# Three low parts of activation combinations moved from VectorE to GpSimd in the first feature group

## The reference

```
    h = h + jnp.concatenate([conv_out, ret_out], axis=-1) @ w_out
    f = jnp.square(jax.nn.relu(rmsnorm(h, norm_ffn_w) @ w_up)) @ w_down
    return h + f, new_hist, new_state.astype(h.dtype)
```

## Time and profile before

| what | value |
|---|---|
| time, median of 3 runs | 1175.36 us (1175.01 to 1176.11) |
| time of the profiled execution | 1177.58 us |
| its span in the profile | 1175.8 us |
| busy PE, PEld | 1161.0 us (99%), 1061.5 us (90%) |
| busy DVE, ACT, POOL | 931.1 us (79%), 548.0 us (47%), 379.9 us (32%) |

### The profile page before, as it was taken

How to read it: one execution, slowest core, us unless ns; L and a number is a source line. 1 busy time by engine, 2 the same in 40 slices (tenths; PEclk the granted TensorE clock), 3 DMA queues, 4 the chain that set the end, 5 groups by cost and what they waited for, 6 DMA issues and landing times.

```text
span 1175.8 us, 20816 instructions
## 1 busy us (share of the span) xinstructions
PE 1161.0 (99%) x6346; PEld 1061.5 (90%) x6346; DVE 931.1 (79%) x1630; ACT 548.0 (47%) x1140; POOL 379.9 (32%) x282
## 2 busy tenths in 40 slices
PE   8999999999999999999999999999999999999998
PEld 6899999999999888979989989988998998998996
DVE  6467796887968754499898898898889889889877
ACT  7544434343254432546435435434534633643556
POOL 3401131112220045344343343343433333334303
PEclk9999999999999999999999999999999999999999
DMA  7631111211121441431021021021012112102204
GB/s 268 185 112 37 41 50 36 65 43 40 49 68 62 144 152 36 152 99 45 28 71 54 18 71 54 27 62 62 27 54 62 40 40 71 54 18 71 62 27 153
DMA packets 99714, 82.66 MB, mean 70 GB/s; under 512 B 9936, under 2 KB 82640, under 8 KB 99680
## 3 DMA queue, kind: packets, MB, share of 16 engines
q1 hardware_dynamic: 99392, 81.47, 22.3%
q10 hardware_dynamic: 288, 0.79, 0.2%
HBM read 70.95 MB, written 11.28 MB: 70 GB/s over the span
## 4 chain that ended last, share of the span: by engine, by line
PE 87%; DVE 6%; DMA 3%; issue 1%; ACT 1%; POOL 1%; SPq 1%; POOLq 0%; DVEq 0%; ACTq 0%
PE pp L2065 27%; PE pp L2067 27%; PE pp L2066 27%; PE pp L2071 1%; PE pp L2072 1%; DMA out<-ncs 1%; DVE wo_lo L1536 1%; PE pp L2085 1%; DMA h<-in_x_prompt 1%; DVE mid_lo L1543 1%; PE pp L2199 1%; PE pp L2188 1%; PE pp L2181 1%; PE pp L2198 1%; DMA xr<-in_x_prompt 0%
## 5 line engine op out<-in xcount | busy, mean ns | idle before, releaser
L1752 DVE TENSOR_TENSOR h<-pp,h 128x512 f32<-128x512 f32 x420 | 267.5, 680 | 6.0 <-PE pp L2067 5.9
L2065 PE MATMUL pp<-do_hi,fo_hi 128*128 128x512 f32 x452 | 177.0, 392 | 2.0 <-DVE fo_lo L1745 2.0
L2067 PE MATMUL pp<-do_hi,fo_lo 128*128 128x512 f32 x452 | 176.4, 390 | 0.0
L2066 PE MATMUL pp<-do_lo,fo_hi 128*128 128x512 f32 x452 | 176.4, 390 | 0.0
L2065 PE MATMUL pp<-mid_hi,fo_hi 128*128 128x384 f32 (+1 forms) x528 | 170.0, 322 | 0.0
L2067 PE MATMUL pp<-mid_hi,fo_lo 128*128 128x384 f32 (+1 forms) x528 | 170.0, 322 | 0.0
L2066 PE MATMUL pp<-mid_lo,fo_hi 128*128 128x384 f32 (+1 forms) x528 | 169.9, 322 | 0.0
L1059 ACT ACTIVATE fo_hi<-fo_flat 128x512 fp32r<-128x512 f32 x124 | 75.7, 625 | 115.9 <-POOL fo_flat L2025 60.9
L1701 DVE TENSOR_TENSOR fo_lo<-fo_flat,fo_hi 128x512 fp32r<-128x512 f32 x124 | 103.2, 854 | 6.3 <-ACT fo_hi L1059 6.3
L2065 PEld LDWEIGHTS pp<-do_hi,fo_hi 128*128 128x128 f32 x452 | 84.8, 188 | 22.8 <-DVE fo_lo L1745 3.1
L2067 PEld LDWEIGHTS pp<-do_hi,fo_lo 128*128 128x128 f32 x452 | 84.9, 188 | 18.1
(11 more groups left out here) (293 smaller groups left out, 2775.5 us busy)
## 6 DMA issues: line engine op xcount, KB each, us to landing
fo_flat<-in_w_up SPq DMA_DIRECT2D x64, 256.0 KB, 2.9
do_raw<-in_w_down SPq DMA_DIRECT2D x49, 256.0 KB, 3.3
i_raw_A<-in_w_in SPq DMA_DIRECT2D x48, 256.0 KB, 3.1
xr<-in_x_prompt SPq DMA_DIRECT2D x8, 512.0 KB, 6.4
do_hraw<-in_w_down SPq DMA_DIRECT2D x15, 256.0 KB, 2.5
tx_raw_T<-tx_parts SPq DMA_DIRECT2D x3, 768.0 KB, 5.9
xt_parts<-fo_hraw SPq DMA_DIRECT2D x9, 256.0 KB, 2.9
xt_raw<-xt_parts SPq DMA_DIRECT2D x3, 768.0 KB, 8.5
```

The lines of the kernel that those rows point to most:

```text
L1752: dve.tensor_tensor(h_part(p, q), bank_of(p, q)[:, :], h_part(p, q), ALU.add).then_inc(dve_add, 1)
L2065: pe.matmul(out, a_hi, b_hi, start=start, stop=False, skip_group_check=again)
L2066: pe.matmul(out, a_hi, b_lo, start=False, stop=False, skip_group_check=again)
L2067: return pe.matmul(out, a_lo, b_hi, start=False, stop=stop, skip_group_check=again)
```

## The change

The low parts of T2, T3 and T4 leave VectorE's `up_first`. GpSimd makes them instead, in its pass for group 0, between the sums of down weights and the sums of features. Group 0 is taken out of GpSimd's loop for that, which then runs over groups 1 to 14. A new semaphore, `xt_early`, counts them, and TensorE waits for it where it uses T2, T3 or T4. The low part of T1 stays on VectorE, where it was.

```
-                xt_lo_part("T2")
-                xt_lo_part("T3")
                 f_low(0, "A11", F_HI)
-                xt_lo_part("T4")
                 f_low(0, "A12", F_HI)
...
-            def group(g):
+            def group(g, first):
...
                 pool.tensor_tensor(d["T4"], d["B21"], d["T2"], ALU.subtract).then_inc(d_sum, 1)
+                if first:
+                    for n, name in enumerate(XT_ORDER[:3]):
+                        pool.wait_ge(xt_hi_ready, n + 1)
+                        pool.tensor_tensor(xt_part(name, xt_lo, mid_lo), xt_part(name, xt_raw, mid_lo_raw),
+                                           xt_part(name, xt_hi, mid_hi).bitcast(F32), ALU.subtract).then_inc(xt_early, 1)
                 pool.wait_ge(fr_ready, 6 * g + 4)
                 pool.tensor_tensor(f_s["S3"], a21, a11, ALU.subtract).then_inc(f_sum_pool, 1)
...
-            with pool.Fori(0, G_LAST) as g:
-                group(g)
+            group(0, True)
+            with pool.Fori(1, G_LAST) as g:
+                group(g, False)
...
-                    pe.wait_ge(xt_ready, XT_ORDER.index(xn) + 1)
+                    if xn == "T1":
+                        pe.wait_ge(xt_ready, 1)
+                    else:
+                        pe.wait_ge(xt_early, XT_ORDER.index(xn) + 1)
```

More of the change, by code:

```diff
@@ L389, in build @@
         xt_ready = sem("xt_ready")
+        xt_early = sem("xt_early")
         f_sum_pool = sem("f_sum_pool")
```

## The result

The changed kernel takes 1184.99 us (median of 6 runs, 1183.74 to 1186.25) where the kernel before takes 1175.41 (6 runs, 1175.01 to 1176.88). The ratio is 1.0078, with a 95% interval of 1.0068 to 1.0088: 9.2 us slower (8.0 to 10.3). The difference of the two medians is 9.6 us; the ratio is an estimate from all runs and not their quotient. The time lies inside the predicted range, 1.8 us above the predicted 1183.2. The profiled execution took 1184.73 us, its span is 1183.0, 7.2 us more than that of the earlier trace rows.

A forecast was written before the change was run, and what follows sets the result against it. TensorE was taken to bound the kernel, with no slack behind it. P1 8.14 us later, less 1.86 given back, plus 1.5 for the low clock made +7.8 us, so 1183.2 us, range 1181.0 to 1186.8.

The forecast's parts named there:

- The chain: Group 0: three GpSimd subtractions delay S3, then S1, A11's low part and P1, which starts 8.14 us later at 511.83.
- The moved instruction: One 128x1536 subtraction on GpSimd was taken to cost 3.5 us, between bounds of 3.45 and 3.90.
- S1's turn: After S3, GpSimd's S1 goes before VectorE's low part of A11, ending at about 511.22; that low part ends at 511.78.
- Given back: TensorE's stops at P2 and the sample products both vanish: -1.86 us, or nearly that.
- The clock: After 9.6 us idle TensorE restarts at the low clock level, 7 matmuls in 3.05 us: +1.5 us.
- The sum: Whole kernel: +6.3 us from the engines plus 1.5 for TensorE's low clock, together +7.8 us.
- put the profile's difference on the median: The profiled span's +7.8 us was added unchanged to the median of 1175.36, giving 1183.2 us.
- rival 2: GpSimd slower than 3.5 us per subtraction, or low clock lasting longer: 1184.4 to 1188.4, around 1186; chance 0.20.
- the clock staying up: TensorE keeps full clock after its stop and the rest holds: +6.3 us, 1181.7; chance 0.17.
- VectorE winning the turn: VectorE's low part of A11 goes before S1, P1 starts 1.1 us earlier: 1182.1 us; chance 0.04.
- no change: S3's delay is absorbed elsewhere, say by a low part of A11 not needing S3; chance 0.03.
- The faster rival: Freed VectorE unblocks GpSimd's S3 if the three subtractions finish before 499.5: -3.3 us, 1172.0; chance 0.03.

The follow-up runs named there:

- f3: Changed kernel with the three GpSimd subtractions moved behind the sum S4, nothing left out: 1180.67 us against 1177.89 for the kernel before, ratio 1.0021.
- g3: Changed kernel with each of the three subtractions cut in four pieces of 128x384, same place: 1186.68 us against 1177.43 for the kernel before, ratio 1.0071.
- f1: The kernel before, unedited, measured and profiled once more: 1177.56 us against 1177.89, ratio 1.0000.
- f2: The changed kernel, unedited, measured and profiled once more beside the kernel before: 1186.07 us, ratio 1.0078.
- e1: Changed kernel with 34 extra matmuls keeping TensorE busy in its stop: 1183.88 us against 1177.18 for the kernel before, ratio 1.0052.
- g4: Changed kernel with 34 extra matmuls in TensorE's stop, measured a second time: 1184.13 us against 1177.43 for the kernel before, ratio 1.0053.
- e2: Changed kernel without the three subtractions, TensorE reading the high parts instead: 1175.31 us against 1177.18 for the kernel before, ratio 0.9985.
- e3: Changed kernel with the three subtractions shortened to 128x384 each, the rest left out: 1178.25 us against 1177.18 for the kernel before, ratio 1.0009.
- f4: Changed kernel, subtractions in 128x384 pieces, T2's and T3's behind S4, T4's behind sums of up weights: 1177.98 us against 1177.89 for the kernel before, ratio 1.0005.
- g1: Changed kernel with T2's low part back on VectorE, T3's and T4's in pieces behind S4: 1176.73 us against 1177.43 for the kernel before, ratio 0.9993.
- g2: Kernel before, all low parts on VectorE, reordered T2, A11, T3, A12, T4: 1177.34 us against 1177.43, ratio 0.9999.

## Why the prediction was right

- **The chain** held link by link. S3 was expected at 508.67 and started at 508.34; P1 at 511.83, and it started at 511.41. By the marks P1 came 7.5 us later in the first pair of profiles and 7.8 in the second, against 8.14 predicted; counted from VectorE's first low part it is 7.7 in both. f3 and g3 show that it is S3's place: moved behind S4 the stop is gone, cut in pieces it is not.
- **The moved instruction** was taken at 3.5 us with 3.45 as the lower bound. Undisturbed it takes 3.41, below that bound: by the rows of 384, 512 and 1536 elements (1.00, 1.30, 3.41 us) a fixed part of about 0.2 us (an estimate) is not repeated, and three times 1.15 counts it three times. The estimate by the Trainium skill's figure (GPSIMD Engine Reference, section 3.1), 3.43, was the better one.
- **S1's turn** went as rows 8 said: S1 at 509.56 ran in 1.25 us, VectorE's two low parts took 3.35.
- **Given back:** 1.86 us predicted. P1 to sample is 7.32 us before and 5.59 with the clock kept up, so 1.73.
- **The clock:** +1.5 predicted; 7.00 - 5.59 = 1.4 us in the first profile, 2.1 in the second.
- **The sum:** +7.8 predicted. The marks give +7.1 and +8.1, the profiled spans +7.2 and (f1, f2) +6.8. The ratios give +9.2 twice, with 7.3 as the lower end of the second; the medians differ by 9.6 and 8.2. The step of the prediction that put the profile's difference on the median is thus the one that is off, by 1 to 2 us in the first measurement and less surely in the second. The profiled execution of before was 2.2 us above its median, and the changed kernel's was not: the stretch ahead of the change's place varies by more than that between executions. Whether the rest is the clock's price in runs that were not profiled (3 us by the ratios of e1 and g4, 1.4 to 2.1 by the profiles; the profiled execution's granted clock, 0.994, is not unlike the 0.993 to 0.995 of the others) or scatter is not settled.
- **The range:** its upper end does not follow from the words given for it. 1184.4 and half again of 1.5 us make 1185.2, half of rival 2's further 4.0 us would make 1186.4, and neither is 1186.8; the measured 1184.99 lies inside each.
- **The rivals:** the clock staying up is excluded by the windows, VectorE winning the turn and no change by the timelines. The second rival was nearest by its time, 1184.4, but half of it is wrong: GpSimd was not slower (11.28 us for the three, where 11.44 were predicted). The low clock lasting longer was seen once, in f2, and gave 0.6 us. The faster rival was right that there are 1.8 to 2.8 us to gain (e2), but its condition could not be met at any length: T4's high part is done at 501.52 in the earlier trace rows, so the three cannot all be done before 499.5. With pieces of 1.0 us instead of 3.4 the loss is near zero (e3), and it is that high part which then holds S3.

## What to carry to other kernels

Before work goes to an engine that is less than half busy, look what stands behind it on that engine's queue at that place: GpSimd was 32% busy and idle for 5 us ahead of S3, but its next sum was due in 2.5 us and the moved work took 11. Work that is wanted 30 us later belongs behind what is wanted next, and on GpSimd perhaps in pieces short enough that VectorE's turn does not wait long: f4 and g1 lose less behind S4 than f3, but they also have a third less work there, so pieces alone were not tested. And a stop of TensorE of some 9 us costs more than itself, 1.4 us or more for the clock.

## What was not expected of the hardware

- The same stop at the same place cost 1.4 us of clock in one execution and 2.1 in another: the level rose 3.0 us after P1 began in the one, 4.6 in the other.
- The first 494 us, identical in all these kernels, took from 492.8 to 498.4 us up to the first low part of a down weight. That is as much as many an edit here is worth, so marks inside the profile told more than spans. In f4, where it took longest, the granted clock fell between 444 and 452 us; in the other profiles it is 1.00 there. Whether that is all of the delay is not shown. The stretch of f4 (columns as above):

```profile
444.00:448.00 4.00, 3.93 (x18) 3.22 (x19) 1.96 (x5) 1.95 (x6) 3.84 (x4) 0.73 0.00 0
```

- After a stop of only 2.1 us the rest of a stage ran 1.6 us longer (g2), while e3 had one of 2.45 us, and f3 one of 1.92, and ran on at full clock.
